# A two-block transformer kernel: a sink column, loads in pieces, an end by token halves, and a new table of durations behind the order of instructions

## What is computed

```
def window_attn_mixer(h, positions, w_in, sink, w_out):        # 16 q heads, 4 kv heads, hd 64
    proj = h @ w_in                                             # q 1024, k 256, v 256 columns
    q = rope(q, positions); k = rope(k, positions)
    scores = einsum('bcqhgd,bckhd->bchgqk', q, k_band) * hd ** -0.5
    scores = where(mask, scores, -inf)
    m = maximum(max(scores, -1), sink)
    p = exp(scores - m[..., None])
    denom = sum(p, -1) + exp(sink - m)
    return (einsum('bchgqk,bckhd->bcqhgd', p, v_band) / denom).reshape(B, S, -1) @ w_out
def swiglu(h, w_in, w_out):                                     # D_FF 2816
    gate, up = split(h @ w_in)
    return (silu(gate) * up) @ w_out
def second_block(x, ...):
    x = x + mlstm_mixer(rmsnorm(x, w0), ...);  x = x + swiglu(rmsnorm(x, w1), ...)
    x = x + window_attn_mixer(rmsnorm(x, w2), ...);  x = x + swiglu(rmsnorm(x, w3), ...)
    return rmsnorm(x, norm_final_w)
```

## Time and profile before

| | |
|---|---|
| median of 3 runs | 1521.32 us (1520.42 to 1522.09) |
| the profiled execution's own time | 1520.36 us |
| its span, first to last instruction | 1518.5 us |
| PE busy | 1467.8 us (97%) |
| DVE busy | 795.6 us (52%) |
| ACT busy | 572.1 us (38%) |
| POOL busy | 37.0 us (2%) |
| mean granted clock of PE | 0.988 |

### The profile page before, as it was taken

One profiled execution on the slowest core, in us unless ns is written; L12 is line 12 of the kernel. 1 busy time (PEld: TensorE's weight loads), 2 busy tenths in 40 slices (PEclk: granted clock), 3 DMA queues, 4 the chain that ended last, 5 costly groups with the idle time before them and its releaser, 6 DMA issues.

```text
span 1518.5 us, 17798 instructions
## 1 busy us (share of the span) xinstructions
PE 1467.8 (97%) x7088; PEld 1191.5 (78%) x7088; DVE 795.6 (52%) x1535; ACT 572.1 (38%) x1024; POOL 37.0 (2%) x43
## 2 busy tenths in 40 slices
PE   7999998999999899999999999999899999999996
PEld 7777765888788678888888878867678888888885
DVE  4665653566655764443344454587655443344443
ACT  5554542344443443222222233366653322222221
POOL 0011000000000000000000000000000000000000
PEclk9999999899999999999999999999999999999998
DMA  6121110131211122222322223210013222322221
GB/s 239 66 74 56 56 56 28 62 119 56 78 62 56 56 84 84 102 75 98 128 84 95 76 83 128 84 56 1 29 56 106 89 94 77 121 99 96 87 81 69
DMA packets 20610, 123.15 MB, mean 81 GB/s; under 512 B 2224, under 2 KB 2352, under 8 KB 9392
## 3 DMA queue, kind: packets, MB, share of 16 engines
q1 hardware_dynamic: 20528, 122.02, 23.3%
HBM read 119.91 MB, written 2.10 MB: 80 GB/s over the span
## 4 chain that ended last, share of the span: by engine, by line
PE 66%; issue 24%; DVE 6%; ACT 3%; DMA 0%; POOL 0%; POOLq 0%; DVEq 0%; SPq 0%; ACTq 0%
PE PS L231 58%; PE PS L246 5%; PE PS L254 3%; DVE FT L227 1%; DVE WL L219 1%; ACT FT L206 1%; ACT WH L206 1%; DVE G L219 1%; DVE FT L223 1%; DVE FT L219 0%; DVE FT L708 0%; DVE FP L227 0%; DVE FR L219 0%; DMA RAW<-in_w_in 0%; ACT FR L206 0%
## 5 line engine op out<-in xcount | busy, mean ns | idle before, releaser
L231 PE MATMUL PS<-XH,WH 128*128 128x512 f32 x1080 | 431.1, 399 | 0.0
L231 PE MATMUL PS<-XH,WL 128*128 128x512 f32 x1080 | 421.5, 390 | 0.0
L231 PE MATMUL PS<-XL,WH 128*128 128x512 f32 x1080 | 421.3, 390 | 0.0
L219 DVE TENSOR_TENSOR WL<-RAW,WH 128x1024 fp32r<-128x1024 f32 (+2 forms) x242 | 263.2, 1129 | 165.0 <-ACT WH L206 162.1
L231 PE MATMUL PS<-FR,WH 128*128 128x512 f32 x1088 | 341.2, 395 | 7.6 <-DVE SC L223 2.7
L206 ACT ACTIVATE WH<-RAW 128x1024 fp32r<-128x1024 f32 (+2 forms) x242 | 223.7, 973 | 146.9 <-PE PS L231 141.8
L231 PEld LDWEIGHTS PS<-FR,WH 128*128 128x128 f32 x1088 | 205.2, 190 | 52.9 <-issue 4.6
L231 PEld LDWEIGHTS PS<-XH,WH 128*128 128x128 f32 x1080 | 203.2, 188 | 48.4 <-issue 7.5
L231 PEld LDWEIGHTS PS<-XH,WL 128*128 128x128 f32 x1080 | 203.1, 188 | 43.2
L231 PEld LDWEIGHTS PS<-XL,WH 128*128 128x128 f32 x1080 | 203.2, 188 | 42.6 <-issue 2.6
L231 PE MATMUL PS<-FR,WL 128*128 128x512 f32 x544 | 213.8, 393 | 0.0
(11 more groups left out here) (113 smaller groups left out, 1241.7 us busy)
## 6 DMA issues: line engine op xcount, KB each, us to landing
RAW<-in_f_in SPq DMA_DIRECT2D x44, 1024.0 KB, 4.8
RAW<-in_w_in SPq DMA_DIRECT2D x13, 1024.0 KB, 4.8
RAW<-in_m_in SPq DMA_DIRECT2D x12, 1024.0 KB, 4.8
RAW<-in_f_oa SPq DMA_DIRECT2D x16, 768.0 KB, 4.1
RAW<-in_f_ob SPq DMA_DIRECT2D x16, 640.0 KB, 3.9
RAW<-in_a_in SPq DMA_DIRECT2D x6, 1024.0 KB, 4.8
RAW<-in_w_out SPq DMA_DIRECT2D x4, 1024.0 KB, 4.9
RAW<-in_m_out SPq DMA_DIRECT2D x4, 1024.0 KB, 4.9
```

The source lines that it names most:

```text
L219: return q.op(lambda e: e.tensor_tensor(o, a, b, op), *after, us=us)
L231: f = lambda e: e.matmul(o, l, r, start=start, stop=stop, skip_group_check=True)
```

## The change

1. Durations: new figures for ACT, DVE and PE, and LAG, the time after an operation's end until its semaphore counts as seen, by engine instead of 0.07 for all.
2. Sink column: the masked minimum starts from the sink instead of a large number and POOL copies the sink into one more column of the scores, so that the exponential's own sum contains it. Gone are a minimum, a subtraction and an addition on DVE and one exponential on ACT per item.
3. A_ORDER: the first q chunk of the attention before the v chunk.
4. Loads: x and chunk 0 in four pieces each, in turn, the first 8 columns of small in between, the rest of it after; warm_up puts 16 float32 matmuls of ONE with itself ahead of everything on PE.
5. End: last_pair computes the last two feature tiles by halves of 256 tokens, four PE tiles, and norms, scales and stores the first half while PE works on the second. The norm's weight is multiplied in beforehand by ACT (G<-XT,SM).

```
+LAG = {"pe": 0.24, "ac": 0.07, "dv": 0.07, "po": 0.1, "sp": 0.07}
-        WHEN[self.name, self.n] = self.t + 0.07
+        WHEN[self.name, self.n] = self.t + LAG[self.name]
 def act(o, i, f, *after, scale=1.0, bias=None, accum=None):
-        us = 0.1 + 0.00083 * width(o) + (0 if accum is None else 0.19)
+        us = 0.19 + 0.00083 * width(o) + (0 if accum is None else 0.19) + (0 if isinstance(scale, float) else 0.09)
...
+    A_ORDER = (0, 2, 1, 3, 4, 5)
...
-        return j, h, l, [w_split[j][0 if k < n0 else 1] for k in range(nk)]
+        return j, h, l, [w_split[j][k * len(w_split[j]) // nk] for k in range(nk)]
+    t_x, t_w0, t_n1 = [], [], None
+    for i in range(4):
+        part = slice(512 * i, 512 * i + 512)
+        t_x.append(load(XT[:, 2 * i:2 * i + 2, :], xv[:, 2 * i:2 * i + 2, :], f"x{i}"))
+        t_w0.append(load(RAW[:, 0, part], chunks[0][0][:, part], f"w0{i}"))
+        if i == 0:
+            t_n1 = load(SM[:, 0:8], A["small"][:, 0:8], "n1")
+    t_sm = load(SM[:, 8:NSMALL], A["small"][:, 8:NSMALL], "sm")
...
+    def warm_up():
+        b, fb = bank.take()
+        for i in range(16):
+            t = mm(PS[:, b, 0:128], ONE[:, :], ONE[:, :], True, True, t_one, fb, last=(i == 15))
+        bank.put(b, t)
     def prep_all(wcol):
-        w_prep(0, (0,))
-        for d in range(KT):
-            prep_parts(d, wcol)
-            if d == 2:
-                w_prep(0, (1,))
+        w_split[0] = []
+        for i in range(4):
+            part = slice(512 * i, 512 * i + 512)
+            w_split[0].append(split(RAW[:, 0, part], WH[:, 0, part], WL[:, 0, part], t_w0[i]))
+            prep_parts(2 * i, wcol)
+            prep_parts(2 * i + 1, wcol)
...
-            for dp in range(4):
+            for dp in range(3 if half == 1 and next_w == C_FIN else 4):
...
+            if half == 1 and next_w == C_FIN:
+                last_pair(hid)
+                return
...
+    def last_pair(hid):
+        YT, oo = G, out.rearrange("(k p) s -> p k s", p=128)
+        cw = lambda d: SM[:, C_FIN + d:C_FIN + d + 1]
+        tm = [copy(YT[:, d, :], XT[:, d, :], st["x"][d], t_sm, st["g", d], scale=cw(d)) for d in range(6)]
+        ws = [w_use(), w_use()]
...
+        def tile(th, u, ks):
+            c, (b, fb) = half[th], bs[2 * th + u]
+            for k in ks:
+                j, h, lo, wt = ws[k // 6]
+                hh, hl, tk = hid[k]
+                t = mm3(PS[:, b, 0:256], (h[:, k % 6, u * 128:u * 128 + 128], lo[:, k % 6, u * 128:u * 128 + 128]),
+                        (FR[:, hh, c], FR[:, hl, c]), k == 0, k == FH - 1, wt[k % 6], tk, fb, last=(k == ks[-1]))
+            if k == FH - 1:
+                x = XT[:, 6 + u, c]
+                t = tt(x, x, PS[:, b, 0:256], ALU.add, t, st["x"][6 + u], xs[6 + u])
+                q, qf = sq[u]
+                sqt[th, u] = act(FT[:, q, c], x, ACT.Square, t, qf)
+                mul[th, u] = copy(YT[:, 6 + u, c], x, t, t_sm, st["g", 6 + u], scale=cw(6 + u))
...
+            for lo, hi in ((0, 4), (4, 6), (6, 8)):
+                y = YT[:, lo:hi, c]
+                r = PS[:, b, 128:384].unsqueeze(1).to_broadcast([128, hi - lo, 256])
+                t3 = tt(y, y, r, ALU.mult, t2, tm, [mul[th, 0], mul[th, 1]] if hi == 8 else None)
+                SP.add(lambda e, y=y, lo=lo, hi=hi: e.dma_start(oo[:, lo:hi, c], y), [t3], (so, 16))
+        every = list(range(FH))
+        tile(0, 0, every)
+        tile(0, 1, every)
+        tile(1, 0, every)
+        n0 = sums(0)
+        tile(1, 1, every[:6])
+        store(0, *n0)
+        tile(1, 1, every[6:])
+        store(1, *sums(1))
...
-                x = DV.op(lambda e, o_=o_, i_=i_, a_=a_: e.tensor_tensor_reduce(
-                    out=o_, in0=i_, in1=mask, scale=1.0, scalar=-NEG, op0=ALU.add, op1=ALU.min, accum_out=a_), t, sf, t_co, us=0.45)
+                sink = nsk[:, hq + g:hq + g + 1]
+                y = PO.op(lambda e, o_=FT[:, s, W:W + 1], i_=sink: e.tensor_copy(o_, i_), tns, sf, us=0.3)
+                o_, i_, a_ = FT[:, s, 0:W], PS[:, b, 0:W], nm[:, g:g + 1]
+                x = DV.op(lambda e, o_=o_, i_=i_, a_=a_, sink=sink: e.tensor_tensor_reduce(
+                    out=o_, in0=i_, in1=mask, scale=1.0, scalar=sink, op0=ALU.add, op1=ALU.min, accum_out=a_),
+                    t, sf, t_co, tns, us=0.23 + 0.00104 * width(o_))
...
-            t4 = act(es, es, ACT.Exp, ta)
-            t = tt(dn, sm, es, ALU.add, t3, t4)
-            t = DV.op(lambda e: e.reciprocal(rd, dn), t)
+            t = DV.op(lambda e: e.reciprocal(rd, sm), t3)
```

More of the change, by code:

```diff
@@ L275, in blocks_kernel @@
     xv = A["xT"].rearrange("(k p) s -> p k s", p=128)
-    t_sm = load(SM[:, :], A["small"], "sm")
-    t_x = [load(XT[:, 2 * i:2 * i + 2, :], xv[:, 2 * i:2 * i + 2, :], f"x{i}") for i in range(1)]
     chunks = []
@@ L1042, in ffn, with sums, store @@
                 fr.put(hl, t)
+    def last_pair(hid):
[3 more added lines that the diff above has]
+        ws = [w_use(), w_use()]
+        bs = [bank.take() for _ in range(4)]
+        bn = [bank.take() for _ in range(2)]
+        sq = [ft.take() for _ in range(2)]
+        so = dsem("out")
+        half = [slice(0, 256), slice(256, 512)]
+        quarter = [slice(128 * i, 128 * i + 128) for i in range(4)]
+        sqt, mul = {}, {}
+        def tile(th, u, ks):
[11 more added lines that the diff above has]
+                mul[th, u] = copy(YT[:, 6 + u, c], x, t, t_sm, st["g", 6 + u], scale=cw(6 + u))
+        def sums(th):
+            (b, fb), rc, m = bn[th], sc(2), sc(2)
+            for i in range(2):
+                mm(PS[:, b, i:i + 1], ACC[:, quarter[2 * th + i]], ONE[:, 0:1], i == 0, False, st["acc"], fb, t_one, last=False)
+            for u in range(2):
+                for i in range(2):
+                    t = mm(PS[:, b, i:i + 1], FT[:, sq[u][0], quarter[2 * th + i]], ONE[:, 0:1], False, u == 1, sqt[th, u],
+                           last=(u == 1 and i == 1))
+            t = ts(m, PS[:, b, 0:2], 1.0 / D, ALU.mult, t, s2=EPS, op1=ALU.add)
+            return rc, rpow(rc, m, 2, t)
+        def store(th, rc, t):
+            b, c = bn[th][0], half[th]
+            for i in range(2):
+                t2 = tr(PS[:, b, 128 + 128 * i:256 + 128 * i], rc[:, i:i + 1].to_broadcast([128, 128]), IDN, t, t_co, last=(i == 1))
+            for lo, hi in ((0, 4), (4, 6), (6, 8)):
[12 more added lines that the diff above has]
+        store(1, *sums(1))
@@ L1531, in a_heads @@
         ft.put(si, st["rope_read"])
+    warm_up()
     prep_all(C_N1)
```

79 lines of the change are left out of this document (28 added, 51 removed).

## The result

The changed kernel took 1527.27 us (median of 5 runs, 1525.52 to 1529.65), the kernel before 1521.32: a ratio of 1.0040, 95% interval 1.0029 to 1.0051. It is slower, by 0.4%, where I had given 0.92 to faster. The profiled run took 1525.52, its span is 1523.7, its mean granted clock 0.982.

A forecast was written before the change was run, and what follows sets the result against it. TensorE, busy 1467.8 of 1518.5 us, was taken as the bound, leaving its idle time and clock loss to win. Terms -3.2 - 1.8 - 8.2 - 8.0 + 5.4 = -15.8 gave 1505.5 us, range 1498.5 to 1513.5.

The forecast's parts named there:

- The start: Kernel start: earlier first weights and half-size splits let PE go on at 21.0 instead of 24.4; -3.2 us.
- First block and mLSTM: First two stages: the recomputed order covers waits with more projection matmuls; -1.8 us in the first block, -8.2 in mLSTM.
- half of it back as new waits: The mLSTM term's lower bound: a gain of only 4 us instead of 8.2.
- The attention stage: Attention block, 940:1120: heads start sooner and rope waits shrink, 3 us of waits and 0.8 of clock left; -8.0 us.
- Two edits meet: Opening of the attention term: only the sink column and the new chunk order act there; together -8.0 us.
- 6 projection matmuls, 1.4 us, now stand in the same place: Attention stage: 6 projection matmuls cover 1.4 us of the 3.09 us wait at 1017.19, which keeps part of it.
- The end: Last pair: six scalings before the last chunk's splits make PE wait 5.1 us, against a shorter tail; +5.4 us.
- (2): Rival: the attention stage keeps its idle time, moved to the 14 items without projections; 1513.5 us, chance 0.2.
- (4): Rival: attention items without projections each wait, at 1.5 us an item 21 us are lost; 1526 us, chance 0.04.
- (3): Rival: POOL's 64 copies, up to 1.01 us each, hold DVE up in the attention stage; 1513 us, chance 0.05.
- (5): Rival: new durations change the order without filling waits, only start and end remain; 1523.5 us, chance 0.04.

The follow-up runs named there:

- e8: The changed kernel with the loads, first splits and start of before, without warm-up; 1527.68 us.
- e6: The changed kernel with all durations and the lag (0.07) of before; chunk order, sink column, loads and end stay; 1518.66 us.
- e14: e10, but from a_proj on only the lag is that of before and the durations stay the new ones; 1519.84 us.
- e16: The kernel before with the new durations and lag alone; 1520.75 us.
- e18: The changed kernel with the edits of e1 and e7, and from a_proj on matmuls on 64 rows priced (w + 32) / 1900; 1507.96 us.
- e2: The changed kernel with 14 unread filler matmuls on PE before the value product that waits 3.81 us in the attention stage; 1519.37 us.
- e3: The changed kernel with rope2 cut in two, its split FR<-FT emitted later, when the tables say DVE's sum is there; 1515.61 us.
- e7: The changed kernel with all of small loaded in one piece in the place of its first 8 columns; 1519.40 us.
- e1: The changed kernel with last_pair's six scalings emitted behind the splits of the last weight chunk; 1512.54 us.
- e5: The changed kernel with the softmax of before: no sink column, no copies on POOL; 1524.52 us.
- e10: The changed kernel with the edits of e1 and e7, and the durations and lag of before from a_proj on; 1505.34 us.
- e11: The changed kernel with the durations and lag of before and the softmax of before; 1524.68 us.

## Why the prediction was wrong, by its steps

**The start**, -3.2: measured +0.8 in the profiled run at the first 512-wide projection (37.10 instead of 36.28), and some -1 over the kernels with the old and the new loads (e8). The step that failed is "so the first half of chunk 1 is ready at 20.8": I added up DVE's work from its first landing on, as if every later piece were there. The first did come earlier (5.20), the second at 9.94. And where I wrote that PE waits for DVE, I put no price of the clock on it: the window 20:30 reads 0.83, 1.7 us lost, in the changed kernel and in 12 of the other 16 with the new loads, 1.00 before.

**First block and mLSTM**, -1.8 and -8.2: from the first 512-wide projection to the first landmark 874.6 became 866.5, -8.1 for my -10.0. The waits that I named are gone; the sizes were off: 5.1 us came in the first block, where I had 1.8 (all 2.8 us of idle time went; for the other 2.3 no wait accounts), and 3.0 in the rest, because the two new waits, 3.54 and 2.73, and a clock of 0.83 in 350:360 took the place of the old ones. My bound "half of it back as new waits" was the right case.

**The attention stage**, -8.0: measured +7.1. This is the step that turned the sign, and what failed is its first sentence, "Two edits meet". Three meet: the new durations, which I followed through the first two stages, recompute the order here too, and I put that at nothing without a reason. With the durations of before (e6) the other two take idle time from 8.2 to 3.9 us and the middle from 579.0 to 572.5, -6.5 for my -8.0 and well inside my bounds. The new durations put 6.1 us of idle time and a clock of 0.94 for 0.99 on top, 13.6 us in all (e6, e14 to e16), most of the idle time by the one price of e18.

Three smaller readings failed with it. "6 projection matmuls, 1.4 us, now stand in the same place": in the changed order none stand there, and the 3.09 us wait became 3.81. "The heads start some 30 projection matmuls sooner" I counted as cover; by the eighth item 87 in-projection matmuls were spent, and 9 were left for the next five (e18). And "I price a wait of 2.5 us or more at 1.7 us on top" was the cheapest case seen, 3.4 us at 1.2 GHz; here it was 14.6 us, 7.3 lost (e2, e3). The wait of 3.47 us did go, but waits of 2.82 and 1.82 came at 1060 and 1111.

That the gain stayed away is the order's; that the sign turned is in part luck. In e7 the same order, with 10.4 us idle for 10.0, had the clock at 0.98 in the stage and not 0.94, and the kernel took 1519.40, as fast as before.

**The end**, +5.4: +5.35, PE's wait 4.86 for the 5.1 forecast, 9.6 us from PE's last projection matmul (1514.09) to the end, and e1 gave 5.75 back by taking away the one cause named. Right.

**The rivals.** (2), the stage keeps its idle time, was nearest in its mechanism, with 10.0 us idle, but only 5.9 of it stood behind the last in-projection matmul (1052.25), and it had no place for the clock. (4) was nearest in its number, 1526, and not in its mechanism: between 1052 and 1102 the items without projections had 2.8 us of idle time in all, not 1.5 each. (3), POOL's copies, is out by e5: 58 copies in 960:1120 took 0.216 us each in the mean, not 1.01, and with the copies gone the middle was the same, 586.4, with more idle time. They read SBUF beside DVE. By the Trainium skill, SBUF — State Buffer, "SBUF: two separate sides", that could hold DVE up where DVE has two SBUF inputs; no run here shows that it did. (5), only start and end remain, 1523.5, had the sign right, but the start brought 1 us or so and the stages up to the first landmark gained 7.3. My 0.04 for each of (4) and (5), and the 0.03 for slower, came from seeing only gains in an order made from better numbers.

## What to carry to other kernels

A table of durations that sets an order must be checked operation by operation against the trace, each shape by itself; here one price, 0.087 us for a matmul that took 0.21, made most of the difference in idle time. The old table's 0.161 for it was too low as well, and its order was the better one: a table with better numbers in most places is not yet a better plan, and each stage that it reorders has to be read again. Of a long wait of TensorE two prices count, the wait and what the clock takes after it; the second can be the greater, and one wait less or a filler in it wins both. A first landing tells nothing about the second: add up what stands in the queue for each piece. And one profile of each kernel doesn't tell 1 us at the start, or 6 us after a long wait, from the chip's own spread: look at the idle time and the clock of the stage first, and at the other kernels that share the edit.

## What the runs showed of the hardware

- The same wait, 3.8 us, in the same order of instructions, was followed by 14.6 us at 1.2 GHz (changed kernel), 12.1 (e1) and 3.4 (e7), with PE at work all the time behind it. What decides it is open. e14, which has this wait, spreads from 1512.5 to 1525.6 in 12 runs, with mean clocks from 0.989 to 0.979; e10, which hasn't, from 1501.9 to 1507.7 in 5.
- The same transfers in the same order land at different times: with the same loads ACT starts the split of the second piece of weights at 7.88 (e6) to 9.95 (e11), 2 us apart. A difference of 0.9 us between two profiles is no sign of a cause.
- DVE's masked minimum takes 615 ns instead of 554 (384 wide) and 481 instead of 422 (256 wide) when its start is read from SBUF and not an immediate: 0.06 us, 64 times.
